# A two-block transformer kernel on one core: the order of groups in the norm stage, and where layer 0 waits for its stores of x

## Chip, cores and metric

The kernel runs on one core of a Trainium2 chip. The metric is the device time of one execution in microseconds (us), the median of several runs. One profiled execution is read for where the time goes.

## What is computed

The reference is a chain of two blocks over x, 512 rows of 1024 float32 numbers. The first block ends in a mixture of experts and a layer norm; the second has two layers (latent attention, neighbourhood attention, a gated merge, an MLP), each of which also reads keys and values of 256 context rows. Cut to what the change touches:

```
y = hierarchical_moe(x, ...)                               # two experts per row, weighed by gate
x = layer_norm(DEEPNORM_ALPHA * x + y, ln2_g, ln2_b)       # end of the first block
for l in range(DEPTH_2):                                   # two layers
    h_c = modulate(rms_norm(x_ctx, g_attn[l]), csh1, csc1)
    gl_c, mq_c, mk_c, mv_c, nq_c, nk_c, nv_c = mixer_proj(h_c, *proj_w)
    h = modulate(rms_norm(x_lat, g_attn[l]), sh1, sc1)
    ... attention over h and the context's keys and values ...
    x_lat = x_lat + gt1 * gated_merge(gl, y_mla, y_na, ...)
    h2 = modulate(rms_norm(x_lat, g_mlp[l]), sh2, sc2)
    x_lat = x_lat + gt2 * squared_relu_mlp(h2, w_ff1[l], w_ff2[l])
```

## The kernel before

Rows are tiled by 128 (P), so x has four row tiles (TT = 4). The program is a sequence of stages. In each, `products` (L233) takes a list of groups. A group is an optional batch of matmuls into one PSUM bank, and work of one engine behind it: "v" is VectorE (DVE), "s" is ScalarE (ACT), "g" is GpSimd (POOL). `products` gives every engine its own groups in the order of the list. An engine never passes a group that isn't ready, so the list's order is the order on each engine, and only counters between engines (`after`, `needs`, `reads`) say when a group may start. Within a group, `link` makes the next instruction wait for the one before it. A group with `dma=True` issues a transfer from its engine's queue; at the end of the list (L310 to L312) the engine that issued it waits until it has landed. A stage ends with a barrier of all engines.

**The norm stage** (`stream_norm`, L2687) lies between the experts and layer 0. Its list has four kinds of work.

- `combine_groups` (L2410): for each row tile t, `sums` on DVE (`add`: x times ALPHA at L2434, two multiply-adds with the gathered rows of the two experts at L2437, statistics at L2439 to L2441), `root` on ACT (L2454), and `last` on DVE (`normalise`, L2446 to L2449). POOL gathers the experts' rows (L2423), SP loads x (L2705) and the gains of the norms.
- `rms_groups` (L2509) for x: a square with its sum and a root on ACT (L2537, L2530), a scaling on DVE (L2543). Then `modulated` (L2752): 32 transposes on PE (L395), copied to `hT`, which layer 0 reads, by DVE (L2599) and ACT (L2596), and `scales` (L2719), the gains that these copies apply.
- `late_context` (L3804): layer 1's keys and values of the context rows: products on PE (L342) whose results ACT moves; the heads' norms of `k` and `nk` (L2536, L2530 on ACT; L2572, L2545, L2548 on DVE); transposes on PE (`head_transposes`, L2773, and L395) which ACT moves; and four saves to DRAM that ACT issues (L3864). It returns two parts, `early` and `late`.
- `stores`: two transfers of the normed x to `x_lat` in DRAM, issued by ACT (L2729).

POOL also writes a padded table of biases here (`pad_bias`, L3003; its copies are at L3021). The order of the list is one line, in which `spread` (L218) interleaves two lists in proportion to their lengths:

```python
products(M, "norm_p", early + spread(first + work, late) + scales + turned + stores, tiles=4, ...)
```

**The end of a layer** (`layer_output`, L3470) keeps x in the buffer `layers_yT`. After the last sums, ACT issues four stores of x to `x_lat` (L3538); the end of the list waits for their landing. The next layer's first stage is `latent_attention` (L2799), whose `stacked` (L2871 to L2873) is a small group on DVE; its scratch `squares` lies in the same `layers_yT`, and the second half of that layer loads x back from `x_lat` at L3500.

Of the kernel before, what the change touches and what calls it, by code (L numbers as in the profile page):

```python
# [16 lines left out]
ALU = mybir.AluOpType  # L17
# [7 lines left out]
TT = T // P  # L25
D = 1024
# [52 lines left out]
class Group:  # L79
# [5 lines left out]
    def __init__(self, pe, evac, on, tile=None, after=(), needs=(), other=None, pool="", reads=(), dma=False):  # L85
        self.dma = dma
        self.pe, self.evac, self.on, self.tile, self.other = pe, evac, on, tile, other
        self.after, self.needs, self.pool, self.reads = tuple(after), tuple(needs), pool, tuple(reads)
# [144 lines left out]
def products(M, name, groups, tiles=0, pools=ALL_BANKS, extra=None):  # L233
# [8 lines left out]
    for g in groups:  # L242
        if g.dma:
            g.landed = sig[f"landed{sum(x.dma for x in groups[:groups.index(g)])}"]
            continue
        tally[g.on] += 1
        g.count = tally[g.on]
        if g.pe:
            g.number = len(made)
            made.append(g)  # L250
            slots, mine = pools[g.pool], used[g.pool]
            g.before = mine[-len(slots)] if len(mine) >= len(slots) else None
            b, n = slots[len(mine) % len(slots)]
            g.bank = M.ps[:, b:b + n, :].rearrange("p b n -> p (b n)")
            mine.append(g)
            if g.tile is not None:
                W.last_group[g.tile] = base + g.number + 1
            if g.other is not None:
                W.last_group[g.other] = base + g.number + 1
# [12 lines left out]
    with nc.Block() as block:  # L272
# [22 lines left out]
        def mover(eng, on):  # L295
# [14 lines left out]
            for g in groups:  # L310
                if g.dma and g.on == on:
                    eng.wait_ge(g.landed, 16)  # L312
# [2097 lines left out]
def combine_groups(M, st, x, yg, loaded):  # L2410
# [21 lines left out]
    def add(dve, link, t):  # L2432
        dve.wait_ge(loaded(t), 16)
        link(dve.tensor_scalar(x[:, t, :], x[:, t, :], ALPHA, None, ALU.mult))  # L2434
        dve.wait_ge(sig[f"y{t}"], 32)
# [7 lines left out]
    def normalise(dve, link, t):  # L2443
# [5 lines left out]
        return dve.tensor_tensor(x[:, t, :], x[:, t, :], g[:, 1, :], ALU.add)  # L2449

    work, made, before = [], [], None
    for t in range(TT):
        sums = group(None, lambda eng, _, link, t=t: add(eng, link, t), "v")
        root = group(None, lambda eng, _, link, t=t: eng.activation(  # L2454
            rs[:, t:t + 1], mv[:, t, 1:2], ACT.Sqrt, bias=M.ln_eps[:, :]), "s", after=(sums,))
        last = group(None, lambda eng, _, link, t=t: normalise(eng, link, t), "v", after=(root,))
        work += [sums, root] + ([before] if before else [])
        before = last
        made.append((last,))
    return work + [before], made, gather, gains  # L2460

# [225 lines left out]
def stream_norm(M, layers, hT):  # L2687
# [5 lines left out]
    with Stage(nc, "norm_in") as st:  # L2693
# [4 lines left out]
        x = yg[:, 0, :, :]  # L2698
        early, late, context_load = late_context(M, st)
        first, made, gather, combine_gains = combine_groups(M, st, x_in, yg, lambda t: sig[f"x{t}"])  # L2700

# [14 lines left out]
        def gain(eng, link, l, n, out):  # L2716
            if l == 0 and n == 0:
# [5 lines left out]
                  for l, L in enumerate(layers) for n, out in ((0, L.gain1), (1, L.gain2))]  # L2723
        work, done = rms_groups(M, st, "rms", x_in, TT, 1, D, made=made, out=x,
                                share=Squares([yg[:, 1, i, :] for i in range(2)]))
# [5 lines left out]
                  for b in range(2)]  # L2731
        products(M, "norm_p", early + spread(first + work, late) + scales + turned + stores, tiles=4,
                 extra={"sync": load, "gpsimd": pool_work})

# [64 lines left out]
def latent_attention(M, L, l, hT, y, sums):  # L2799
# [9 lines left out]
    with Stage(nc, f"mla{l}") as st:  # L2809
# [61 lines left out]
        def stacked(dve, _, link):  # L2871
            dve.wait_ge(small_landed, (4 + 2 * TT) * 16)
            return dve.tensor_reduce(pick, M.ident[:, :].rearrange("p (q n) -> p n q", q=4), AX, ALU.add)  # L2873
        picked = group(None, stacked, "v")
# [595 lines left out]
def layer_output(M, layers, l, hT, y):  # L3470
# [6 lines left out]
    with Stage(M.nc, f"out{l}") as st:  # L3477
# [21 lines left out]
        final = [blocks[0][4][-1], blocks[1][4][-1]]  # L3499
        loaded = [group(None, lambda act, _, link, t=t: act.dma_start(x[:, t, :], stream_rows(M, t)), "s",  # L3500
                        reads=(final[t // 2],), dma=True) for t in range(TT)]
        complete = [(blocks[1][a][-3], blocks[1][a][-1], blocks[1][b][-3], blocks[1][b][-1]) for a, b in ((0, 2), (1, 4))]
# [31 lines left out]
        def target(t):  # L3534
            if last:
# [3 lines left out]
                        dma=True) for t in range(TT)]  # L3539
        if not last:  # L3540
            nxt = layers[l + 1]
            xn2 = flat[:, 2 * BANK:2 * BANK + TILE].rearrange("p (t d) -> p t d", d=D)
# [261 lines left out]
def late_context(M, st):  # L3804
# [37 lines left out]
    ups = []  # L3842
# [13 lines left out]
    for b in k_turned:  # L3856
# [8 lines left out]
             for dst, src, of in ((M.ctx_v[1], v[:, :, :].rearrange("p t n -> p (t n)"), ups),  # L3865
                                  (M.ctx_k[1], kT[:, :, :].rearrange("p h n -> p (h n)"), k_turned),
                                  (M.ctx_nv[1], nv[:, :, :].rearrange("p t n -> p (t n)"), vs),
                                  (M.ctx_nk[1], nkT[:, :, :].rearrange("p k n -> p (k n)"), nk_turned))]
    return kv + rest + low_work + ks + turned + ups + vs, k_work + nk_work + k_turned + nk_turned + saves, load

# [33 lines left out]
def program(nc, A, out):  # L3904
    M = Machine(nc, A, out)
    with ExitStack() as ctx:
# [41 lines left out]
        M.weights = Weights(nc, ring, tiles, slots, nc.alloc_semaphore(name="groups_done"))  # L3948
        M.scratch_L = nc.dram_tensor("scratch_L", [4, T], F32).ap()
        M.ctx_h = nc.dram_tensor("ctx_h", [P, DK * CTX], F32).ap()  # L3950
        M.x1 = nc.dram_tensor("x1_rows", [T, D], F32).ap()
# [84 lines left out]
```

## Time and profile before

| | us |
|---|---|
| median of 3 runs | 4245.66 (4245.24 to 4246.1) |
| profiled execution, its own time | 4244.85 |
| its span, first to last instruction | 4243.1 |
| PE busy | 3769.9 (89%) |
| DVE busy | 1747.2 (41%) |
| ACT busy | 757.3 (18%) |
| POOL busy | 163.2 (4%) |

The span is what the profile's rows cover; the 1.75 us beside it in the same execution lie outside the first and last instruction. Start times in the rows count from the span's start. PE is TensorE's matmul, PEld its weight load, SP the engine that issues most transfers. A busy share is an average over the whole program; in the stretches that the change touches the shares are quite different.

### The profile page before, as it was taken

The numbers are of one execution on the slowest core, as the hardware profiler recorded it, in microseconds if no ns is written. First come the engines' busy times: TensorE is split into PE (matmuls) and PEld (weight loads), VectorE is DVE, ScalarE is ACT, GpSimd is POOL, SyncE is SP. The second block draws the span as 40 slices with busy tenths as digits, with TensorE's granted clock in tenths as the row PEclk, the third lists the DMA queues.
The fourth block names the chain that finished last, engine by engine and source line by source line (L and its number), as shares of the span: only waits on it lengthen the run. The fifth ranks groups of instructions, "written<-read, shape, count | busy, mean of one in ns | idle before, by whom it ended". The sixth has DMA issues, their size and how long they took to land. (4 is left out here: it accounts for less than half of the span.)

```text
span 4243.1 us, 38455 instructions
## 1 busy us (share of the span) xinstructions
PE 3769.9 (89%) x14796; PEld 2141.4 (50%) x14796; DVE 1747.2 (41%) x3047; ACT 757.3 (18%) x1690; POOL 163.2 (4%) x377
## 2 busy tenths in 40 slices
PE   7988777799578999999866899999998899999999
PEld 3653663444344343555433555448744455447844
DVE  0128643344513211111115556355446556445545
ACT  0212201111012211000112434110001354211000
POOL 1001000000000000000020300000000300000000
PEclk9988777799689999999987999999999999999999
DMA  7443001223166768888742201132222201122221
GB/s 298 169 158 111 1 5 50 95 93 129 71 227 266 290 245 344 338 352 343 292 179 68 90 21 60 70 109 80 80 79 85 102 21 60 42 98 80 80 79 60
DMA packets 197193, 574.69 MB, mean 135 GB/s; under 512 B 24324, under 2 KB 34356, under 8 KB 183752
## 3 DMA queue, kind: packets, MB, share of 16 engines
q1 hardware_dynamic: 177704, 518.35, 32.5%
q10 hardware_dynamic: 11424, 27.37, 1.9%
q0 software_dynamic: 7888, 26.53, 1.7%
q8 instruction: 121, 1.98, 0.2%
q14 instruction: 56, 0.46, 0.0%
HBM read 540.49 MB, written 31.73 MB: 135 GB/s over the span
## 5 line engine op out<-in xcount | busy, mean ns | idle before, releaser
L342 PE MATMUL ps<-out_sums 128*128 128x256 f32 (+1 forms) x1152 | 333.6, 450 | 2.3 <-issue 2.3
L342 PE MATMUL ps<-mixers_xT,ring 128*128 128x512 f32 (+2 forms) x928 | 306.9, 491 | 1.7 <-PEq L272 0.9
L342 PEld LDWEIGHTS ps<-out_sums 128*128 128x128 f32 x1152 | 218.7, 190 | 114.2 <-issue 94.5
L342 PEld LDWEIGHTS ps<-mixers_xT,ring 128*128 128x128 f32 (+1 forms) x928 | 173.5, 188 | 130.4 <-issue 115.2
L342 PE MATMUL ps<-ring,mixers_xT 128*128 128x512 f32 (+2 forms) x608 | 222.7, 524 | 9.9 <-DVE ab_qk L336 6.1
L342 PE MATMUL ps<-ring,layers_hT 128*128 128x512 f32 x416 | 186.7, 606 | 25.5 <-PEq L272 23.5
L2205 PE MATMUL ps<-ring,moe_xgT 128*64 128x512 f32 x432 | 192.0, 601 | 3.0 <-issue 2.2
L342 PEld LDWEIGHTS ps<-ring,mixers_xT 128*128 128x128 f32 x608 | 119.9, 211 | 109.1 <-issue 94.1
L342 PE MATMUL ps<-ring,out_hidden 128*128 128x512 f32 x384 | 167.4, 592 | 0.0
L2206 PE MATMUL ps<-ring,moe_xgT 128*64 128x512 f32 x368 | 163.1, 598 | 0.0
L342 PEld LDWEIGHTS ps<-ring,layers_hT 128*128 128x128 f32 x416 | 79.6, 194 | 126.8 <-issue 122.7
L342 PE MATMUL ps<-out_hidden 128*128 128x512 f32 x288 | 125.7, 593 | 6.2 <-issue 6.2
L2205 PEld LDWEIGHTS ps<-ring,moe_xgT 128*64 128x64 f32 x432 | 58.7, 139 | 127.8 <-issue 127.8
L342 PE MATMUL ps<-layers_hT,ring 128*128 128x256 f32 x512 | 115.3, 387 | 5.1 <-ACT out_rms_rs L2530 5.1
L342 PEld LDWEIGHTS ps<-ring,out_hidden 128*128 128x128 f32 x384 | 73.0, 190 | 91.0 <-issue 90.9
L2205 PE MATMUL ps<-ring,moe_hT 128*64 128x512 f32 x224 | 100.5, 602 | 15.3 <-ACT moe_hT L334 11.3
L2243 DVE TENSOR_TENSOR moe_h<-moe_sg,ps 128x512 f32<-128x512 f32 x16 | 11.0, 688 | 246.7 <-PE ps L2206 246.7
L342 PE MATMUL ps<-ring,layers_yT 128*128 128x512 f32 x256 | 112.5, 592 | 0.0
L342 PEld LDWEIGHTS ps<-layers_hT,ring 128*128 128x128 f32 x512 | 99.5, 195 | 19.7 <-issue 5.5
L430 PE MATMUL ps<-mla_kT,mla_qT 96*128 96x512 f32 (+1 forms) x256 | 96.8, 502 | 8.1 <-ACT mla_S L444 6.6
L342 PE MATMUL ps<-ring,mla_qT 128*128 128x512 f32 (+1 forms) x256 | 94.3, 527 | 8.3 <-DVE mla_qT L2598 6.3
L342 PE MATMUL ps<-ring,ctx_ins 128*128 128x512 f32 (+1 forms) x232 | 95.8, 572 | 0.8 <-ACT ctx_ins L2595 0.8
(895 smaller groups left out, 6157.8 us busy)
## 6 DMA issues: line engine op xcount, KB each, us to landing
ring<-in_w_ff SPq DMA_DIRECT2D x45, 2048.0 KB, 12.9
ring<-in_w_in SPq DMA_DIRECT2D x40, 2048.0 KB, 12.8
ring<-in_e_down SPq DMA_DIRECT2D x27, 2048.0 KB, 8.9
ring<-in_e_gate SPq DMA_DIRECT2D x25, 2048.0 KB, 15.4
ring<-in_e_up SPq DMA_DIRECT2D x25, 2048.0 KB, 11.5
ring<-in_w_ada SPq DMA_DIRECT2D x24, 2048.0 KB, 11.6
ring<-in_w_out SPq DMA_DIRECT2D x8, 2048.0 KB, 11.4
deep_ring_more<-in_e_gate SPq DMA_DIRECT2D x8, 2048.0 KB, 16.7
```

Of the source, the lines that this page charges most:

```text
L342: last = pe.matmul(out, lhsT, rhs, start=(j == 0), stop=(j == len(pairs) - 1))
L430: last = pe_.matmul(bank[:, e * BANK + c0:e * BANK + c0 + n], q, k, start=True, stop=True)
L2205: pe.matmul(bank[0:HALF, :], left(k)[:, 0:HALF], wa[:, k, cols], **ends)
L2206: last = pe.matmul(bank[HALF:P, :], left(k)[:, HALF:P], wb[:, k, cols], **ends)
L2243: lambda eng, bank, link, i=i: eng.tensor_tensor(h[:, i, :], sg[:, i, :], bank, ALU.mult),
```

## The change

The norm stage: `late_context` now returns its parts one by one, the weighing of x by ALPHA becomes four groups of its own, and the list is written out by hand instead of by one `spread`. The number of instructions on each engine stays the same. Layer 0's four stores of x get a semaphore of their own, `M.x_stored`, and are left out of the wait at the end of the list; layer 1 waits for it in `stacked`, ahead of the first use of the buffer as scratch, and in `load_rows`, ahead of the reads of `x_lat`.

```diff
@@ __init__ of Group, products
-        self.dma = dma
+        self.dma, self.awaited = dma, None
...
-            g.landed = sig[f"landed{sum(x.dma for x in groups[:groups.index(g)])}"]
+            g.landed = g.awaited or sig[f"landed{sum(x.dma for x in groups[:groups.index(g)])}"]
...
-                if g.dma and g.on == on:
+                if g.dma and g.on == on and g.awaited is None:
                     eng.wait_ge(g.landed, 16)
@@ combine_groups
     def add(dve, link, t):
-        dve.wait_ge(loaded(t), 16)
-        link(dve.tensor_scalar(x[:, t, :], x[:, t, :], ALPHA, None, ALU.mult))
         dve.wait_ge(sig[f"y{t}"], 32)
...
+    def weigh(dve, t):
+        dve.wait_ge(loaded(t), 16)
+        return dve.tensor_scalar(x[:, t, :], x[:, t, :], ALPHA, None, ALU.mult)
...
+    weighed = [group(None, lambda eng, _, link, t=t: weigh(eng, t), "v") for t in range(TT)]
-        sums = group(None, lambda eng, _, link, t=t: add(eng, link, t), "v")
+        sums = group(None, lambda eng, _, link, t=t: add(eng, link, t), "v", after=(weighed[t],))
...
-    return work + [before], made, gather, gains
+    return weighed, work + [before], made, gather, gains
@@ stream_norm
-        early, late, context_load = late_context(M, st)
+        (low, keys, ups, values, heads, heads_turned, saves), context_load = late_context(M, st)
...
-        products(M, "norm_p", early + spread(first + work, late) + scales + turned + stores, tiles=4,
-                 extra={"sync": load, "gpsimd": pool_work})
+        scaled_, squares = [g for g in squares if g.on == "v"], [g for g in squares if g.on == "s"]
+        sums, roots, lasts = [first[i] for i in (0, 2, 5, 8)], [first[i] for i in (1, 3, 6, 9)], [m[0] for m in made]
+        work = weighed + low + keys[0:1] + [sums[0], roots[0], *scales] + keys[1:] + [sums[1], roots[1], lasts[0]] + ups
+        work += [squares[0], sums[2], roots[2], lasts[1], *heads[:3], squares[1], *values[0:1]]
+        tail = [scaled_[0], sums[3], roots[3], lasts[2], *values[1:], squares[2], scaled_[1], lasts[3], squares[3], *scaled_[2:]]
+        work += spread(tail, heads[3:]) + stores + heads_turned + saves + turned
+        products(M, "norm_p", work, tiles=4, extra={"sync": load, "gpsimd": pool_work})
@@ latent_attention, stacked
             dve.wait_ge(small_landed, (4 + 2 * TT) * 16)
+            if l:
+                dve.wait_ge(M.x_stored, 16 * TT)
@@ layer_output
-        loaded = [group(None, lambda act, _, link, t=t: act.dma_start(x[:, t, :], stream_rows(M, t)), "s",
-                        reads=(final[t // 2],), dma=True) for t in range(TT)]
+        def load_rows(act, t):
+            if l:
+                act.wait_ge(M.x_stored, 16 * TT)
+            return act.dma_start(x[:, t, :], stream_rows(M, t))
+        loaded = [group(None, lambda act, _, link, t=t: load_rows(act, t), "s", reads=(final[t // 2],), dma=True)
+                  for t in range(TT)]
...
         if not last:
+            for store in stores:
+                store.awaited = M.x_stored
@@ late_context
-    return kv + rest + low_work + ks + turned + ups + vs, k_work + nk_work + k_turned + nk_turned + saves, load
+    return (kv + rest + low_work, ks, turned + ups, vs, k_work + nk_work, k_turned + nk_turned, saves), load
```

What the list's new order does to the engines is shown at three places. PE's own sequence, POOL's and SP's are the same as before. Line numbers behind the change are its own: L2434 is now L2451, L2437 is L2435, and the rest lies some lines lower.

**Place 1: DVE from the context's low-rank norm on.** Names: `x_in` is x, `yg` the gathered experts' rows, `c_k` the context's keys, `layers_gain` the modulating gains. Before:

```order
L2543 TENSOR_SCALAR norm_in_c_ckv<-norm_in_c_ckv,norm_in_c_ckv_rs 128x256
L2434 TENSOR_SCALAR norm_in_x_in<-norm_in_x_in 128x1024
L2437 SCALAR_TENSOR_TENSOR norm_in_x_in<-norm_in_yg,gate,norm_in_x_in 128x1024 x2
L2439 BN_STATS norm_in_stats<-norm_in_x_in 128x6
L2440 BN_STATS norm_in_stats<-norm_in_x_in 128x6
L2441 BN_AGGR norm_in_mv<-norm_in_stats 128x2
L2572 TENSOR_REDUCE norm_in_c_k_ss<-norm_in_c_sq 128x8
L2434 TENSOR_SCALAR norm_in_x_in<-norm_in_x_in 128x1024
```

Now:

```order
L2451 TENSOR_SCALAR norm_in_x_in<-norm_in_x_in 128x1024 x4
L2546 TENSOR_SCALAR norm_in_c_ckv<-norm_in_c_ckv,norm_in_c_ckv_rs 128x256
L2435 SCALAR_TENSOR_TENSOR norm_in_x_in<-norm_in_yg,gate,norm_in_x_in 128x1024 x2
L2437 BN_STATS norm_in_stats<-norm_in_x_in 128x6
L2438 BN_STATS norm_in_stats<-norm_in_x_in 128x6
L2439 BN_AGGR norm_in_mv<-norm_in_stats 128x2
L2722 SCALAR_TENSOR_TENSOR layers_gain_0<-mod,norm_in_g 128x16 x2
L2722 SCALAR_TENSOR_TENSOR layers_gain_1<-mod,norm_in_g 128x16 x2
L2435 SCALAR_TENSOR_TENSOR norm_in_x_in<-norm_in_yg,gate,norm_in_x_in 128x1024 x2
```

The four weighings stand ahead of the context's low-rank norm. Behind the first tile's statistics came the sum over `c_sq`, which needs the context's keys; now the gains and the second tile follow at once.

**Place 2: ACT behind the last product `ups` of the context.** `c_nv` are values, moved from PSUM; `c_sq` with `c_k` is the square that DVE's first sum over `c_sq` needs. Before:

```order
L334 ACTIVATE norm_in_c_nv<-ps 128x512 x2
L2536 ACTIVATE norm_in_c_sq<-norm_in_c_k 128x768
L2454 ACTIVATE norm_in_ln_rs<-norm_in_mv,ln_eps 128x1
L2536 ACTIVATE norm_in_c_sq<-norm_in_c_k 128x768
L2530 ACTIVATE norm_in_c_k_rs<-norm_in_c_k_ss,eps 128x8
L2454 ACTIVATE norm_in_ln_rs<-norm_in_mv,ln_eps 128x1
L2530 ACTIVATE norm_in_c_k_rs<-norm_in_c_k_ss,eps 128x8
```

Now:

```order
L2540 ACTIVATE norm_in_yg,norm_in_rms_ss<-norm_in_x_in 128x1024
L2533 ACTIVATE norm_in_rms_rs<-norm_in_rms_ss,eps 128x1
L2457 ACTIVATE norm_in_ln_rs<-norm_in_mv,ln_eps 128x1
L2539 ACTIVATE norm_in_c_sq<-norm_in_c_k 128x768 x2
L2540 ACTIVATE norm_in_yg,norm_in_rms_ss<-norm_in_x_in 128x1024
L2533 ACTIVATE norm_in_rms_rs<-norm_in_rms_ss,eps 128x1
L334 ACTIVATE norm_in_c_nv<-ps 128x512
L2533 ACTIVATE norm_in_c_k_rs<-norm_in_c_k_ss,eps 128x8
L2457 ACTIVATE norm_in_ln_rs<-norm_in_mv,ln_eps 128x1
```

The roots and squares of the first tiles of x stand ahead of the moves of `c_nv`.

**Place 3: ACT at the end of the list.** Before:

```order
L2530 ACTIVATE norm_in_rms_rs<-norm_in_rms_ss,eps 128x1
L2595 ACTIVATE norm_in_c_nkT<-ps,norm_in_c_col_gain 128x256 x3
L3864 DMA ctx_v<-norm_in_c_v 128x1024
L3864 DMA ctx_k<-norm_in_c_kT 96x2048
L3864 DMA ctx_nv<-norm_in_c_nv 128x1024
L3864 DMA ctx_nk<-norm_in_c_nkT 128x1024
L2596 ACTIVATE layers_hT<-ps,mod,layers_gain_0 128x8x64 x4
L2729 DMA x_lat<-norm_in_x_in 256x1x1024 x2
```

Now:

```order
L2533 ACTIVATE norm_in_c_nk_rs<-norm_in_c_nk_ss,eps 128x8
L2732 DMA x_lat<-norm_in_x_in 256x1x1024 x2
L334 ACTIVATE norm_in_c_kT<-ps 96x256 x8
L2598 ACTIVATE norm_in_c_nkT<-ps,norm_in_c_col_gain 128x256 x4
L3880 DMA ctx_v<-norm_in_c_v 128x1024
L3880 DMA ctx_k<-norm_in_c_kT 96x2048
L3880 DMA ctx_nv<-norm_in_c_nv 128x1024
L3880 DMA ctx_nk<-norm_in_c_nkT 128x1024
L2599 ACTIVATE layers_hT<-ps,mod,layers_gain_0 128x8x64 x4
```

The stores of x moved ahead of the moves of the transposed heads (`c_kT`, `c_nkT`) and of the four saves; before, they were the last thing in the list (behind the copies to `layers_hT`).

## Rows read from the trace of the kernel before

**Rows 1.** Windows of the norm stage (us, busy us per engine, PE clock, DMA share, GB/s):

```profile
2220.00:2230.00 10.00, 0.00 (x0) 0.00 (x0) 9.69 (x15) 1.12 (x3) 0.00 (x0) 0.50 0.00 0
...
2280.00:2290.00 10.00, 10.00 (x24) 4.45 (x23) 6.17 (x4) 1.19 (x2) 0.00 (x0) 0.98 0.49 114
```

**Rows 2.** Timeline of DVE in the norm stage (start us, us, work, [idle before <-releaser]):

```profile
2182.57 0.69 DVE L2434 TENSOR_SCALAR norm_in_x_in<-norm_in_x_in 128x1024 f32<-128x1024 f32 x1
...
2187.25 0.21 DVE L2441 BATCH_NORM_AGGREGATE norm_in_mv<-norm_in_stats 128x2 f32<-128x12 f32 x1
2216.62 0.95 DVE L2572 TENSOR_REDUCE norm_in_c_k_ss<-norm_in_c_sq 128x8 f32<-128x768 f32 x1 [29.16 <-ACT norm_in_c_sq L2536]
...
2244.34 0.63 DVE L2572 TENSOR_REDUCE norm_in_c_nk_ss<-norm_in_c_sq 128x8 f32<-128x512 f32 x1
...
2246.57 0.15 DVE L2446 RECIPROCAL norm_in_ln_rs<-norm_in_ln_rs 128x1 f32<-128x1 f32 x1
...
2253.45 0.15 DVE L2541 RECIPROCAL norm_in_rms_rs<-norm_in_rms_rs 128x1 f32<-128x1 f32 x1
...
2256.90 0.42 DVE L2719 SCALAR_TENSOR_TENSOR layers_gain<-mod,norm_in_g 128x16 f32<-128x16 f32 x4
```

**Rows 3.** Timeline of PE, norm stage and start of layer 0:

```profile
2230.88 3.65 PE L2773 MATMUL ps<-ident,norm_in_c_k 128*96 128x128 f32 x16 [15.66 <-DVE norm_in_c_k L2548]
...
2257.38 6.61 PE L395 MATMUL ps<-ident,norm_in_yg 128*128 128x128 f32 x32 [8.64 <-DVE layers_gain L2719]
2276.38 15.98 PE L342 MATMUL ps<-ring,layers_hT 128*128 128x512 f32 x32 [12.39 <-PEq L272]
```

**Rows 4.** Timeline of ACT and its queue (ACTq) in the norm stage:

```profile
2192.95 0.60 ACT L334 ACTIVATE norm_in_c_nk<-ps 128x512 f32<-128x512 f32 x1 [6.27 <-PE ps L342]
...
2202.14 0.39 ACT L334 ACTIVATE norm_in_c_v<-ps 128x256 f32<-128x256 f32 x1
...
2246.19 1.05 ACT L2537 ACTIVATE norm_in_yg<-norm_in_x_in 128x1024 f32<-128x1024 f32 x1
...
2247.57 0.36 ACT L334 ACTIVATE norm_in_c_kT<-ps 96x256 f32<-96x256 f32 x1
...
2256.70 1.93 ACTq L3864 DMA_DIRECT2D ctx_nk<-norm_in_c_nkT  x1
...
2262.80 2.50 ACT L2596 ACTIVATE layers_hT<-ps,mod,layers_gain 128x512 f32<-128x512 f32 x2 [0.42 <-PE ps L395]
2264.03 1.27 ACTq L2729 DMA_DIRECT2D x_lat<-norm_in_x_in  x2
```

**Rows 5.** Loads of the modulating gains (L2709): instruction form and time to landing:

```profile
L2709 SPq DMA_DIRECT2D norm_in_g<-in_g_mlp x2: 554/882/1209, 2167.7 to 2169.0; - x2
...
DMA to landing us min/median/max: 18.5/18.6/18.7
```

**Rows 6.** Landing of the two stores of x (L2729), and a window during them:

```profile
DMA to landing us min/median/max: 7.1/9.0/11.0
...
2269.00:2270.00 1.00, 0.00 (x0) 0.00 (x0) 0.00 (x0) 0.00 (x0) 0.00 (x0) 0.50 1.01 205
```

**Rows 7.** Landing of the four saves of the context (L3864):

```profile
DMA to landing us min/median/max: 2.8/6.1/6.8
```

**Rows 8.** POOL beside DVE: bias copies; four small operations alone; the same four beside DVE:

```profile
2187.03 4.61 POOL L3021 COPY norm_in_rpb_runs<-norm_in_rpb 8x248 f32<-8x248 f32 x8 [12.65 <-DMA norm_in_rpb<-in_rpb]
...
2357.24 1.15 POOL L2558 TENSOR_TENSOR layers_yT<-mla_heads,mla_rope 128x64 f32<-128x64 f32 x4
...
2365.44 2.58 POOL L2558 TENSOR_TENSOR layers_yT<-mla_heads,mla_rope 128x64 f32<-128x64 f32 x4 [4.22 <-DVE mla_heads L2548]
```

**Rows 9.** From layer 0 to layer 1: ACT's queue, SP's queue, landing of the stores (L3538):

```profile
3259.02 2.02 ACTq L3538 DMA_DIRECT2D x_lat<-layers_yT  x2
...
3265.17 2.94 SPq L2838 DMA_DIRECT2D mla_rope<-in_rope_cos  x4
...
DMA to landing us min/median/max: 2.6/4.0/4.8
```

More of the change, by code:

```diff
@@ L2698, in stream_norm @@
         x = yg[:, 0, :, :]
-        early, late, context_load = late_context(M, st)
-        first, made, gather, combine_gains = combine_groups(M, st, x_in, yg, lambda t: sig[f"x{t}"])
+        (low, keys, ups, values, heads, heads_turned, saves), context_load = late_context(M, st)
+        weighed, first, made, gather, combine_gains = combine_groups(M, st, x_in, yg, lambda t: sig[f"x{t}"])
         def load(sp):
@@ L2723, in stream_norm @@
                   for l, L in enumerate(layers) for n, out in ((0, L.gain1), (1, L.gain2))]
-        work, done = rms_groups(M, st, "rms", x_in, TT, 1, D, made=made, out=x,
+        squares, done = rms_groups(M, st, "rms", x_in, TT, 1, D, made=made, out=x,
                                 share=Squares([yg[:, 1, i, :] for i in range(2)]))
@@ L3949, in program @@
         M.scratch_L = nc.dram_tensor("scratch_L", [4, T], F32).ap()
+        M.x_stored = nc.alloc_semaphore(name="x_stored")
         M.ctx_h = nc.dram_tensor("ctx_h", [P, DK * CTX], F32).ap()
```

## The prediction, made before the changed kernel ran

> **What bounds the kernel now.** I read the page first: PE is busy 89% of the span, so only places where PE stands still can give much. The windows of the norm stage show one: from 2220 to 2230 us PE does nothing while DVE is busy 9.69 of 10 us [rows 1]. The timeline of DVE then shows two halves of this stage. After the first tile's statistics, which end at 2187.46, DVE stands idle 29.16 us, until ACT has squared the context's keys; from 2216.62 on it has no pause until the gains end at 2257.32 [rows 2]. So the work on x sits behind a group that becomes ready late, although its data isn't missing. PE's transposes of x begin behind it, at 2257.38, and layer 0's products at 2276.38 [rows 3]. What fills the time between the last copy of the transposes (2265.3 [rows 4]) and 2276.38 is the landing of the two stores of x: the second is issued at 2264.7 and lands at most 11.0 us later, 2275.7 [rows 4, 6], 0.7 us ahead of PE. The second place is the end of layer 0: ACT's last issue ends at 3261.04, the slowest landing took 4.8 us, and the next stage begins at 3265.17 [rows 9].
>
> **DVE's chain in the new order.** No work is removed. DVE's work in the stage behind the context's low-rank norm is what it does without a pause from 2216.62 to 2257.32, 40.7 us, and the first tile's, 4.9 us from 2182.57 to 2187.46 [rows 2]: 45.6. The four weighings (0.69 each [rows 2], 2.8) go ahead of it, into time in which DVE waited anyway: 42.8 remain. Two waits come in. The gains stand behind the first tile's sums, at 2182.57 + 4.2 = 2186.8; their last load is issued at 2169.0 and takes 18.7 [rows 5], so DVE waits until 2187.7, 0.9 us. The first sum over the context's squares then comes behind three tiles' sums (4.2 each), two normalisations (3.44 each, from 2246.57 to 2253.45 for two [rows 2]) and the gains (0.4): at 2203.4. ACT is later: it ends the moves of the context's values at 2202.53 [rows 4], I add 0.3 for a root that now stands ahead of them behind the move at 2192.95, then comes a square of x (1.4, from 2246.19 to 2247.57 [rows 4]), a root and a square of the keys (together about 1.0): 2205.2. DVE waits 1.8. The chain ends at 2182.57 + 42.8 + 0.9 + 1.8 = 2228.1, and I take 2228.5 for a third, short wait for ACT's last square.
>
> **PE and ACT behind it.** The context's last transposes are 8, at 16 in 3.65 us [rows 3] 1.8 us: 2230.3. Then the transposes of x, 6.6 us [rows 3]: 2236.9, against 2264.0 before. PE stays at the lower clock there in both kernels, as the 0.50 in the window says [rows 1].
>
> **The transfers decide the end.** Behind the last normalisation DVE has left two scalings (0.86 each, from 2253.45 to 2256.90 for four), and a sum and two scalings of `c_nk` (2.2, from 2244.34 to 2246.57) [rows 2], and the short wait: the last tile of x is normed at about 2224.2, ACT's square and root of it end at 2225.9, and then ACT issues the stores. Alone they took 11.7 us from the first issue (2264.03) to the last landing (2275.7), and the 16 DMA engines were full meanwhile (1.01 at 205 GB/s) [rows 4, 6]. So they land at 2237.6. The four saves are issued from about 2231, into full engines. Before, they took from about 2255.0 to 2256.70 + 6.8 = 2263.5 at most, 8.5 us [rows 4, 7]; less 1 us of start, which overlaps, 7.5 go behind the stores: 2245.1. ACT's own four copies to `hT` (1.25 each, 5.0 [rows 4]) come behind the issue of the saves, the last of which took 1.93 us [rows 4]. That issue may stretch while the queue is full, at most until the stores have landed: 2237.6 + 5.0 = 2242.6, still ahead of the transfers. From landing to PE's first product it was 0.7 us: 2245.8 against 2276.4, **30.6 us earlier**. Bounds: if stores and saves share the engines better than one behind the other, ACT's copies end the stage at the earliest, 2231 + 3.6 of issues + 5.0 = 2239.6, and the gain is 36. The other bound is the next item.
>
> **DVE beside POOL.** DVE works where it stood idle, and there POOL copies biases, 8 copies in 4.61 us, twice [rows 8]. Where both are busy in layer 0, the same four small operations of POOL took 2.58 us instead of 1.15 [rows 8]. So they do hinder each other, and the row shows POOL paying. POOL has time: 16 copies, each as much as 1 us later, end near 2226, long before 2245. For DVE the trace gives no price in this stage. It is between nothing and all of POOL's copies, 2 x 4.61 = 9.2 us; I take 1.0, since the nearest row shows POOL as the one that waits. The Trainium skill (SBUF — State Buffer, Who interferes with whom) says that the pair of ports which the two share is locked for a whole instruction, and that whoever starts first makes the other block. By that rule DVE pays for each copy that gets in first, in the worst order the 9.2 us; the slower small operations agree with a lock, and no row decides who would start first here.
>
> **The end of layer 0.** Four stores are no longer awaited there. Their issue remains: ACT is done at 3261.04 [rows 9]. What is left is the barrier. From the latest landing (3259.0 to 3259.8 + 4.8, so 3263.8 to 3264.6) to the start at 3265.17 it was 0.6 to 1.4 us [rows 9]. So layer 1 starts at 3261.6 to 3262.4, 2.8 to 3.6 us earlier; I take 3.3 and 2.0 as the lower bound, since the stores now share the engines with layer 1's first loads. The two waits that come in cost nothing. `stacked` stands in layer 1's list behind 16 us of products (before layer 0 the first of them took 15.98 [rows 3]), and the loads of x stand in a later stage, while the stores land within 5. If that cover were gone, DVE's queue would wait for at most the 4.8 us of the landing.
>
> **Sum.** 30.6 - 1.0 + 3.3 = 32.9 us. Layer 0 and layer 1 shift whole: their weights are asked for as PE gives slots back, and the window behind layer 0's start shows the DMA engines half busy, 0.49 [rows 1]. Against the profiled execution's own 4244.85 that is 4212.0; it stands 0.8 below the median of 4245.66. From the median it is 4212.8, and I forecast **4213**.
>
> **Rivals.**
> 1. *Stores and saves overlap, ACT's copies end the stage:* gain 36 and 3.6, 4206. For it: 205 GB/s at full engines is no high rate [rows 6], and no row shows both kinds of transfer at once. Against it: 1.01 of the engines is full.
> 2. *DVE pays for POOL's copies* in full, 9.2 us instead of 1.0, and the boundary gives its lower bound: 4213 + 8.2 + 1.3 = 4222.5. The lock of the page named above is this case. For it: DVE has hardly a gap between 2187 and 2229. Against it: in the nearest rows it is POOL that waits.
> 3. *The change moves the wait without shortening it:* a load of weights further on takes back what layer 0 gains, so that the end moves by less than 8 us: about 4240. For it: the last of the ring's loads before layer 0 are as early as before, in either kernel. Against it: PE at 2276.38 waited for the barrier and for no transfer [rows 3], and later loads hang on PE's own progress.
> 4. *Slower, by PE's clock:* layer 0 starts earlier but at the lower of the two levels, 1.2 instead of 2.4 GHz, and stays there. Each us of dense products at that level costs half a us, so the 32.9 us are lost after 66 us at 0.50; with 90 us it would be 4258. For it: the clock is 0.50 all through the stretch before [rows 1], and PE does less in it than before. Against it: before, it was back at 0.98 within 4 us of layer 0's start [rows 1, 3], after just such an idle stretch.
>
> **How the numbers follow.** Forecast 0.80; rival 1 0.07; rival 2 0.07; rival 3 0.03; rival 4 0.02; 0.01 for what I don't see. The range reaches from rival 1 to rival 2, 4206 to 4223, both the bounds of the unknown costs; it leaves out rivals 3 and 4 and the edges of the others. Within 0.2% (8.5 us, about what a measurement of this kernel can tell from no change) lies rival 3; forecast and rivals 1 and 2 are faster. Faster 0.95, same 0.03, slower 0.02.
>
> **What would show it.** In the new profile DVE's idle of 29 us is gone, with two waits of 1 to 2 us in its place; the chain ends near 2228; PE transposes x from about 2230; the stores of x are issued near 2226, and PE's first product of layer 0 is at 2245 to 2247 with SP just ahead of it. Between the first products of layer 0 and of layer 1 nothing but the 3.3 us changes. I am wrong if layer 0 starts after 2250, if the last thing before it is a compute instruction rather than a landing, or if its first 10 us are at 0.50.

## The result and the profile after

| | before | after |
|---|---|---|
| median of the runs beside each other, us | 4245.45 (4242.62 to 4246.1, 4 runs) | 4216.83 (4213.43 to 4219.15, 4 runs) |
| ratio, 95% interval | | 0.9933 (0.9916 to 0.995) |
| the profiled execution's own time, us | 4244.85 | 4215.68 |
| its span, us | 4243.1 | 4213.8 |

The kernel is 28.6 us faster by the medians, 29.3 by the spans; 32.9 were forecast, and the time lies in the range. A second measurement at the end, six runs, gave 4215.52 and a ratio of 0.9932 (0.992 to 0.9944).

I cut both spans at the same five instructions: the first load of the norm stage, PE's first product of layer 0, the end of ACT's last store of layer 0, PE's first product of layer 1, the end.

| us | before | after | saved |
|---|---|---|---|
| up to the norm stage's first load | 2160.82 | 2162.35 | -1.5 |
| norm stage | 115.56 | 86.27 | 29.3 |
| layer 0 to its last store's issue | 984.66 | 986.84 | -2.2 |
| from there to layer 1 | 4.37 | 0.80 | 3.6 |
| layer 1 | 977.69 | 977.54 | 0.15 |

DVE's timeline in the norm stage, after (columns as in [rows 2]):

```profile
2173.64 3.43 DVE L2451 TENSOR_SCALAR norm_in_x_in<-norm_in_x_in 128x1024 f32<-128x1024 f32 x2 [33.77 <-DMA norm_in_x_in<-x_rows]
...
2188.99 1.31 DVE L2722 SCALAR_TENSOR_TENSOR layers_gain<-mod,norm_in_g 128x16 f32<-128x16 f32 x4 [0.84 <-DMA norm_in_g<-in_g_mlp]
2190.23 3.25 DVE L2435 SCALAR_TENSOR_TENSOR norm_in_x_in<-norm_in_yg,gate,norm_in_x_in 128x1024 f32<-128x1024 f32 x2
...
2198.36 2.60 DVE L2435 SCALAR_TENSOR_TENSOR norm_in_x_in<-norm_in_yg,gate,norm_in_x_in 128x1024 f32<-128x1024 f32 x2
...
2204.70 1.54 DVE L2447 TENSOR_TENSOR norm_in_x_in<-norm_in_x_in,norm_in_ln 128x1024 f32<-128x1024 f32 x1
2206.66 0.95 DVE L2575 TENSOR_REDUCE norm_in_c_k_ss<-norm_in_c_sq 128x8 f32<-128x768 f32 x1 [0.42 <-ACT norm_in_c_sq L2539]
...
2208.39 3.23 DVE L2435 SCALAR_TENSOR_TENSOR norm_in_x_in<-norm_in_yg,gate,norm_in_x_in 128x1024 f32<-128x1024 f32 x2
...
2230.00 0.69 DVE L2548 TENSOR_TENSOR norm_in_c_nk<-norm_in_c_nk,norm_in_c_nk_rs 128x512 f32<-128x512 f32 x1
```

The first two weighings take 3.43 us instead of 2 x 0.69 while POOL clears its table beside them (2173.32 to 2175.92): the first takes 2.83 and ends 0.55 us behind POOL. They stand ahead of the chain, and DVE waits for the next rows behind them anyway. The wait of 29.16 us for the context's squares [rows 2] is now 0.42. The same pair of L2435 takes 2.60 when DVE is alone and 3.23 to 3.25 while POOL copies; the statistics in the same stretches (L2437, L2438) keep their 0.69 and 0.68. POOL pays as well: 8 copies took 4.61 [rows 8], now, in its timeline,

```profile
2188.45 6.66 POOL L3031 COPY norm_in_rpb_runs<-norm_in_rpb 8x248 f32<-8x248 f32 x8 [12.53 <-DMA norm_in_rpb<-in_rpb]
...
2203.81 8.86 POOL L3031 COPY norm_in_rpb_runs<-norm_in_rpb 8x248 f32<-8x248 f32 x8 [2.09 <-DMA norm_in_rpb<-in_rpb]
```

Then ACT and its queue, and PE, after; they answer to [rows 3, 4]:

```profile
2227.75 0.60 ACTq L2732 DMA_DIRECT2D x_lat<-norm_in_x_in  x1
...
2233.14 2.15 ACTq L3880 DMA_DIRECT2D ctx_k<-norm_in_c_kT  x1
2235.34 2.44 ACTq L3880 DMA_DIRECT2D ctx_nv<-norm_in_c_nv  x1
2237.82 1.93 ACTq L3880 DMA_DIRECT2D ctx_nk<-norm_in_c_nkT  x1
2239.80 4.33 ACT L2599 ACTIVATE layers_hT<-ps,mod,layers_gain 128x512 f32<-128x512 f32 x4 [6.57 <-issue]
```

```profile
2232.51 4.30 PE L395 MATMUL ps<-ident,norm_in_yg 128*128 128x128 f32 x32
2248.62 16.79 PE L342 MATMUL ps<-ring,layers_hT 128*128 128x512 f32 x32 [11.81 <-PEq L272]
```

ACT's copies end at 2244.13, PE begins at 2248.62. The window from 2229, where the first store's bytes begin to move, to 2246 (columns as in [rows 1]), and the landings of the stores of x and of the saves:

```profile
2229.00:2246.00 17.00, 6.06 (x40) 5.82 (x40) 5.93 (x9) 8.37 (x16) 0.00 (x0) 0.70 0.97 258
```

```profile
DMA to landing us min/median/max: 7.1/9.8/12.4
...
DMA to landing us min/median/max: 9.3/10.7/12.3
```

And of the last save, `ctx_nk`, alone:

```profile
DMA to landing us min/median/max: 10.1/10.1/10.1
```

The DMA engines are busy for 0.97 of 17 us. `ctx_nk`, issued at 2237.82, lands at 2247.9, and PE begins 0.7 us later, just as it did behind the last store of x before (2275.7 and 2276.38 [rows 3, 4, 6]). The transfers end the stage, as they did before; they only begin earlier.

The end of layer 0 (ACT's queue; SP's; PE), after, against [rows 9]:

```profile
3233.44 2.02 ACTq L3552 DMA_DIRECT2D x_lat<-layers_yT  x2
```

```profile
3236.02 3.44 SPq L2846 DMA_DIRECT2D mla_rope<-in_rope_cos  x4
```

```profile
3236.26 9.34 PE L342 MATMUL ps<-ring,layers_hT 128*128 128x512 f32 x16 [3.82 <-PEq L272]
```

SP goes on 0.56 us behind the last issue (3235.46) instead of 4.13, while the slowest store still takes 5.9 us to land.

### The profile page after: what moved, and what is told of

Read it like the earlier page. It is cut to its first block and busy times, and to the rows that moved or that the text cites. A ratio compares the mean times of both kernels' runs of the same rounds, so it can differ in the third digit from the quotient of the medians.

```text
span 4213.8 us, 38458 instructions
## 1 busy us (share of the span) xinstructions
PE 3772.1 (90%) x14796; PEld 2140.0 (51%) x14796; DVE 1751.3 (42%) x3047; ACT 756.8 (18%) x1690; POOL 169.5 (4%) x377
```

## The experiments

Ten more kernels ran, one execution each; `thirds` and the kernel after were then timed again. "Norm stage" and the other stages are cut as in the table above; times counted from the stage's first load are written +66.0. Single executions scatter by some us (before alone: 4238.6 to 4253.4 in the last eleven runs), so I read the stages and not the total where less than 5 us matter.

| kernel | time, us | span | norm stage | layer 0 | to layer 1 |
|---|---|---|---|---|---|
| order_only | 4216.54 | 4214.6 | 86.55 | 986.61 | 4.35 |
| stores_only | 4239.58 | 4237.8 | 115.59 | 984.78 | 0.80 |
| stores_last | 4213.01 | 4211.2 | 89.00 | 984.26 | 0.80 |
| weigh_back | 4213.87 | 4212.0 | 88.96 | 987.99 | 0.80 |
| early_stores | 4222.18 | 4220.3 | 99.10 | 984.41 | 0.78 |
| saves_pool | 4210.85 | 4209.1 | 86.81 | 986.72 | 0.81 |
| no_pad | 4213.19 | 4211.2 | 86.96 | 986.73 | 0.76 |
| stores_up | 4239.25 | 4237.5 | 112.82 | 984.07 | 4.34 |
| halves | 4203.19 | 4201.3 | 81.14 | 982.65 | 0.77 |
| thirds | 4203.26 | 4201.5 | 77.21 | 985.85 | 0.81 |
| thirds_timed | 4205.50 (5 runs) | 4200.9 | 77.86 | 984.67 | 0.77 |
| after_timed | 4215.52 (6 runs) | 4216.7 | 86.28 | 987.19 | 0.76 |

**The two parts, each alone.** order_only is the kernel after without its way of awaiting layer 0's stores:

```diff
-            for store in stores:
-                store.awaited = M.x_stored
-            if l:
-                dve.wait_ge(M.x_stored, 16 * TT)
-            if l:
-                act.wait_ge(M.x_stored, 16 * TT)
```

> The new order of the norm stage alone; layer 0's stores of x are awaited at the list's end again. If the two parts are independent: from the first load of the norm stage to PE's first product of layer 0 it takes 86.3 us as in the changed kernel (115.6 before), and from ACT's last issue of layer 0 to PE's first product of layer 1 4.4 us as before (0.8 in the changed kernel). Rival: the second part depends on the first (both queues of stores share the engines with what follows), then the 4.4 us come out over 1 us different. Total about 3.6 us over the changed kernel's, plus or minus 3 by the clock.

stores_only is the kernel before with those lines and the new attribute `awaited` alone.

> The kernel before with layer 0's stores awaited where layer 1 needs them. Norm stage 115.6 us as before; 0.8 us from ACT's last issue to PE's first product of layer 1. Rival: without the wait the stores share the engines with layer 1's first loads, and layer 1's first groups on DVE come later than before, counted from the stage's start, so that part of the 3.6 us is given back; then the first 100 us of layer 1 are over 1 us longer.

The norm stage is 86.55 with the order and 115.59 without; the boundary 4.35 without the awaiting and 0.80 with it. Each part does its share by itself, 29.0 and 3.6 us, and they don't touch each other. PE's first products of layer 1, in order_only and in stores_only:

```profile
3237.43 7.92 PE L342 MATMUL ps<-ring,layers_hT 128*128 128x512 f32 x13 [7.38 <-PEq L272]
```

```profile
3260.17 8.25 PE L342 MATMUL ps<-ring,layers_hT 128*128 128x512 f32 x13 [3.84 <-PEq L272]
```

**Inside the order.** stores_last puts the stores of x back to the end of the list, behind the transposes of x:

```diff
-        work += spread(tail, heads[3:]) + stores + heads_turned + saves + turned
+        work += spread(tail, heads[3:]) + heads_turned + saves + turned + stores
```

> The changed kernel with the two stores of x back at the end of the norm stage's list, behind ACT's copies to hT. Theory A (the gain comes from DVE's order, and the stores' place only overlaps the transfers): ACT copies end near 2241, the stores are issued then and take 11.7 us, PE starts layer 0 about 4 us later than in the changed kernel, 90 to 91 us after the first load. Theory B (the gain is the overlap of the stores' landing with work): most of the 29.3 us is lost, over 105 us.

weigh_back puts each weighing right before its tile's sums, as it stood before:

```diff
-        work = weighed + low + keys[0:1] + [sums[0], roots[0], *scales] + ...
+        work = low + keys[0:1] + [weighed[0], sums[0], roots[0], *scales] + ...
```

> The changed kernel with each weighing of x again right ahead of its tile's sums. Theory A: DVE's chain bounds the stage, so the four times 0.7 us come back on it; the first is partly hidden, PE starts layer 0 2 to 3 us later (88 to 89 us). Rival: the chain has slack because transfers end the stage; then they move with the last tile's store all the same unless the saves alone bound it: no change within 0.5 us.

stores_up is the kernel before with one line changed, the stores of x ahead of the gains and of the transposes of x:

```diff
-            spread(first + work, late) + scales + turned + stores,
+            spread(first + work, late) + stores + scales + turned,
```

> The kernel before with the two stores of x ahead of the gains and of x's transposes, behind the saves, and nothing else. Theory A: the gain of the place alone is the overlap of the stores with transposes and copies, PE starts layer 0 about 5 us earlier than before, 109 to 112 us after the first load (115.6). Theory B (the place is the cause of most of the gain): under 100 us.

Each of the three is worth 2.7 us (89.00, 88.96, and 112.82 against 115.56). For stores_last that is 1 us less than expected, for stores_up 0.8 us short of the expected range. So of the 29.3 us, 2.7 come from where the stores stand, 2.7 from the weighings in time that DVE spent waiting (four of 0.69 each), and the rest, some 24 if the three add, from DVE's remaining order, which was not taken apart further. That the stores' place is worth so little with DVE's chain shortened is because the saves fill the DMA engines in the stores' stead: stores_last issues its last save 3.3 us earlier (+72.21 against +75.47) and the second store of x 10 us later (+76.04 against +66.04), and its last landing is 2.7 us later (+88.3 against +85.6). In its ACT rows the issue of the stores also overlaps ACT's copies without holding them:

```profile
2231.63 2.03 ACTq L3880 DMA_DIRECT2D ctx_nk<-norm_in_c_nkT  x1
2233.70 1.26 ACT L2599 ACTIVATE layers_hT<-ps,mod,layers_gain 128x512 f32<-128x512 f32 x1 [3.29 <-PE ps L395]
2234.27 1.15 ACTq L2732 DMA_DIRECT2D x_lat<-norm_in_x_in  x1
```

**Does DVE pay for POOL's copies (rival 2)?** no_pad leaves the copies of the bias rows out (the padded table then holds only zeros), and with them everything POOL computes beside DVE's chain (its clearing of the table, ahead of the chain, stays):

```diff
-            for r in range(ROWS):
+            for r in range(0):
```

> The changed kernel without POOL's 16 copies of biases in the norm stage (left out, so that the bias table holds zeros). If POOL's copies cost DVE what its longer instructions show (gains 1.3 instead of 0.4 us, three others 0.3 to 0.65 more each, 2.5 us in all), DVE's chain and with it the stores and PE's first product come 2 to 2.5 us earlier (84 us). Rival: the longer instructions are slowed by transfers or by the table of clocks, not by POOL: no change.

Alone, DVE's rows are short again, and its wait for ACT has grown:

```profile
2186.12 0.43 DVE L2722 SCALAR_TENSOR_TENSOR layers_gain<-mod,norm_in_g 128x16 f32<-128x16 f32 x4 [0.65 <-DMA norm_in_g<-in_g_mlp]
2186.47 2.60 DVE L2435 SCALAR_TENSOR_TENSOR norm_in_x_in<-norm_in_yg,gate,norm_in_x_in 128x1024 f32<-128x1024 f32 x2
...
2203.75 0.95 DVE L2575 TENSOR_REDUCE norm_in_c_k_ss<-norm_in_c_sq 128x8 f32<-128x768 f32 x1 [2.25 <-ACT norm_in_c_sq L2539]
```

In the kernel after, POOL costs DVE 0.88 on the gains, 0.65, 0.32 and 0.63 on the rows shown: 2.5 us. Of these 1.8 only take the place of the wait for ACT (0.42 against 2.25), so x is stored 0.55 us earlier without them (+65.49 against +66.04). The stage isn't shorter at all (86.96; 84 was expected): the last save lands 11.3 us behind its issue instead of 10.1, at +86.3 instead of +85.6. Why it does so stays open. Rival 2 is out: the price is real, a quarter of its bound, and nearly all of it was covered.

**What ends the stage?** early_stores meant to spread the transfers: one store for each tile of x as soon as it is normed, and each save as soon as its data is there.

```diff
-        stored = M.x_lat.rearrange("(c t b) d -> b c t d", b=2, t=TT)
-        stores = [... act.dma_start(stored[b], x_in[b * GRID_W:(b + 1) * GRID_W, 0:TT, :]), ... for b in range(2)]
+        stored = M.x_lat.rearrange("(c t b) d -> t b c d", b=2, t=TT)
+        stores = [... act.dma_start(stored[t], x_in[:, t, :]), ... after=made[t] ... for t in range(TT)]
```

> The changed kernel with the transfers out of the norm stage's tail: the stores of x are four, one per row tile, issued as each tile is normed, and three of the four saves are issued as soon as their data is ready. If transfers end the stage (stores and saves one behind the other, 20 us from the first issue to the last landing), then only one store and one save (512 KB each) are left behind 2228, ACT's copies to hT or the last landing end near 2239, and PE starts layer 0 about 77 us after the stage's first load, 9 us earlier than in the changed kernel (86.3). Rival: the stage is ended by DVE's chain and ACT's copies, or ACT's queue is held up by each issue: then under 4 us.

It missed by 22 us. ACT's queue, DVE and a window of it:

```profile
2215.95 11.38 ACTq L3883 DMA_DIRECT2D ctx_nv<-norm_in_c_nv  x1
2227.38 0.30 ACT L2533 ACTIVATE norm_in_c_nk_rs<-norm_in_c_nk_ss,eps 128x8 f32<-128x8 f32 x1 [11.33 <-issue]
```

```profile
2231.81 0.16 DVE L2544 RECIPROCAL norm_in_rms_rs<-norm_in_rms_rs 128x1 f32<-128x1 f32 x1 [7.87 <-ACT norm_in_rms_rs L2533]
```

```profile
2220.00:2226.00 6.00, 1.30 (x7) 0.83 (x5) 3.87 (x5) 0.00 (x0) 0.00 (x0) 0.50 0.13 53
```

While only stores of the new form were under way, the engines' share was 0.13, at 53 GB/s, where the stores of the kernel after fill them at 200. A share of 0.13 is that of two busy engines out of 16, and 2 is also the outer size of the new destination (`b`), where the other stores have 64 (`c`); that the one follows from the other was not tested. The issue behind them held ACT for 11.38 us, and DVE with it (7.87 us). The stage's last landing, of `ctx_nk`, comes at 2256.6, 19.6 us behind its issue instead of 10.1, and 0.7 us ahead of PE. So this run says nothing on early stores as such, only on this form: all 128 partitions of one tile, in one transfer, to rows interleaved in pairs.

saves_pool lets POOL issue the four saves; the first line is needed for POOL to run a list of transfers alone:

```diff
-            if tally["g"]:
+            if any(g.on == "g" for g in groups):
...
-            ... act.dma_start(dst, src), "s", after=of, dma=True)
+            ... act.dma_start(dst, src), "g", after=of, dma=True)
```

> The changed kernel with the four saves issued by POOL instead of ACT. ACT's copies to hT no longer wait behind issues that take 2 us each, and end about 6 us earlier (77.5 + 4.3 us after the first load in the changed kernel). If the transfers end the stage, layer 0 still starts at 86.3 us, within 1 us; if ACT's blocked issue does, it starts up to 6 us earlier.

POOL, ACT and windows of it:

```profile
2228.90 0.54 POOL L3880 DMA_DIRECT2D ctx_nk<-norm_in_c_nkT  x1 [0.82 <-ACT norm_in_c_nkT L2598]
```

```profile
2229.67 4.38 ACT L2599 ACTIVATE layers_hT<-ps,mod,layers_gain 128x512 f32<-128x512 f32 x4 [1.06 <-PE ps L395]
```

```profile
2236.00:2238.00 2.00, 0.00 (x0) 0.00 (x0) 0.00 (x0) 0.00 (x0) 0.00 (x0) 0.54 0.98 352
2238.00:2240.00 2.00, 0.00 (x0) 0.00 (x0) 0.00 (x0) 0.00 (x0) 0.00 (x0) 0.50 0.73 285
```

ACT's copies end 5.2 us earlier (+76.57 against +81.78), the last save is issued 4 us earlier, and the stage lasts 86.81, as before. In its last 10 us no engine computes. So neither ACT nor the issues set the end: from the first store of x the engines have some 17 us of work (2 MB of x at 200 GB/s, 10.5, and 2.25 MB of saves at about 350, 6.7). In saves_pool `ctx_v` went out 11 us ahead of the stores, and the last landing is 0.9 us earlier than in the kernel after (+84.7 against +85.6). That is lost again behind it. `ctx_nk`, the last save, and PE's first products in saves_pool:

```profile
DMA to landing us min/median/max: 13.3/13.3/13.3
```

```profile
2244.29 16.70 PE L342 MATMUL ps<-ring,layers_hT 128*128 128x512 f32 x32 [12.04 <-PEq L272]
```

It lands at 2242.2, and PE begins 2.1 us later. The same two distances stand in every run: from the stage's last landing to PE it is 0.7 us in the nine kernels where ACT issued that transfer and waits for it, and 2.1 us in saves_pool, halves and thirds, where POOL does. So POOL's part in the end of the stage costs 1.4 us. saves_pool was fast in its time (4210.85) only because its norm stage began 4.9 us earlier than that of the kernel after, which the change doesn't touch.

**Work moved ahead of the full stretch.** halves is saves_pool with `ctx_nv` saved ahead of `ctx_k`, and with the stores of x split by tiles, each still from 64 partitions:

```diff
-        stores = [... act.dma_start(stored[b], x_in[b * GRID_W:(b + 1) * GRID_W, 0:TT, :]), ...
-                  for b in range(2)]
+        stores = [... act.dma_start(stored[b][:, lo:hi, :], x_in[b * GRID_W:(b + 1) * GRID_W, lo:hi, :]), ...
+                  after=sum(made[lo:hi], ()), dma=True)
+                  for lo, hi in ((0, 2), (2, TT)) for b in range(2)]
-        work += [..., *heads[:3], squares[1], *values[0:1]]
+        work += [..., *heads[:3], squares[1], *stores[0:2], *values[0:1]]
-        work += spread(tail, heads[3:]) + stores + ...
+        work += spread(tail, heads[3:]) + stores[2:] + ...
```

> The kernel after with the four context saves issued by POOL (as in the earlier run), ctx_nv ahead of ctx_k, and the two stores of x cut in four: rows of tiles 0 and 1 behind squares[1], rows of tiles 2 and 3 where both stood; each still takes one half of the partitions. Theory (once DVE's chain is short, the stage's end is set by the DMA engines, busy without a gap from the first store of x to the last save, about 17 us; only work moved ahead of that stretch shortens it): 1 MB of x (5.2 us at the 200 GB/s of the stores) moves to about 2204 to 2210 and ctx_nv (1.5 us) ahead too; the stretch starts at the same place and is 10 us long; the norm stage lasts 80 to 82 us instead of 86.3 to 86.8, time about 4205, span 4203 to 4206. Rival A (the last copies of the transposed x, or POOL's last landing, end the stage whatever the engines do): no shorter than 84.5 us, time 4208 or more. Rival B (any store of x ahead of the norm's end slows DVE or blocks ACT's queue, as the per-tile stores did): DVE's chain over 1 us longer than in the run with POOL's saves, ACT's issue over 2 us, time 4212 or more.

thirds splits them at `((0, 2), (2, 3), (3, TT))`, with the middle two behind `squares[2]`.

> The kernel of the run before with tile 2's rows of x in two stores of their own behind squares[2] (512 KB), so that only tile 3's rows (512 KB, 2.6 us at 200 GB/s) are left for the end. Theory: another 2.6 us off the stretch, norm stage 77.5 to 79.5 us, span 4200 to 4203, unless the copies of the transposed x (which ended 76.6 us behind the first load when POOL had the saves) come last: then 79 to 80. Rival A: same as the run before it within 0.5 us. Rival B (stores of one row of 4 KB for each of 64 partitions are as slow as the per-tile ones, 53 GB/s): the DMA share in their stretch is 0.2 to 0.3 and the stage is longer than in the run before it, over 84 us.

Norm stages of 81.14 and 77.21 us: the theory's numbers for the first (80 to 82), 0.3 below them for the second, whose step is 3.9 us instead of 2.6. Both rivals are out; a store of one row of 4 KB for each of 64 partitions still moves at full speed. In thirds: PE, a window behind ACT's last work but one, and the landing of the last save, which POOL issued at 2231.37:

```profile
2230.36 4.39 PE L395 MATMUL ps<-ident,norm_in_yg 128*128 128x128 f32 x32
2237.39 13.09 PE L342 MATMUL ps<-ring,layers_hT 128*128 128x512 f32 x26 [2.64 <-PEq L272]
```

```profile
2235.00:2237.00 2.00, 0.00 (x0) 0.00 (x0) 0.86 (x1) 1.56 (x2) 0.00 (x0) 1.00 0.00 0
```

```profile
DMA to landing us min/median/max: 3.9/3.9/3.9
```

The last save lands at 2235.3, and PE starts 2.1 us behind it, once more. ACT's last copy ends at 2236.56, 0.8 us ahead of PE, with the DMA engines empty. In the second trace of thirds that distance is 1.4 us, and the one from the landing is 2.1 again. So the landing that POOL waits for still ends the stage, and compute comes close behind it. Such stores with ACT issuing the saves were not tried.

**The faster version timed, beside the kernel after.**

> The kernel thirds again, timed in five rounds against the kernel before. By its stages (norm stage 77.2 against 115.6, boundary 0.8 against 4.4, layer 0's own time 1 to 3 us longer where the clock falls behind PE's pause, layer 1 the same) 38.4 + 3.6 - 1.5 = 40.5 us less than before: 4203 to 4206 us, ratio 0.990 to 0.991. Rival (the short stage of one profile was a lucky one, other runs are like the run with POOL's saves alone): 4210.

> The kernel after unchanged, timed beside the one above on the same chip, so that what its own median (4216.8, single times from 4213.4 to 4219.2) holds of chance is known. Theory: its stages say 29.3 + 3.6 - 2.2 = 30.7 less than before by the profile, so 4213 to 4217. The run above is 9 to 12 us faster. Rival (the second measurement lies as high as the first single times): 4218 or more.

Both times hold; the ratio of thirds_timed is just above the expected 0.991. thirds_timed: 4205.50 us, ratio to before 0.9915 (0.9902 to 0.9927). after_timed: 4215.52 us, 0.9932 (0.992 to 0.9944). The norm stages differ by 8.4 us, the medians by 10.0. Single runs of one kernel differ by 8 us and more (after: 4210.85 to 4218.85; before by up to 15), so the difference of the medians is good to some us only; the stages say what it is made of.

## Why the prediction was right, and where its numbers were off

Before the change, the last landing of a transfer ended the norm stage, and DVE's chain decided when the transfers could begin. The forecast's steps, in its order, times again from the stage's first load (2160.82 before, which the forecast's times imply; 2162.35 after):

1. *DVE's chain.* It was to end at 2228.5, with 1.0 for POOL beside it 2229.5, which is +68.7; it ended at 2230.69, +68.34. Two terms were off and nearly cancel: the price for POOL was 2.5 instead of 1.0, and the wait for ACT's squares 0.42 instead of 1.8. They aren't independent: a slower DVE arrives later and waits less. The prediction added them as if they were. no_pad shows the exchange. That the chain came out within 0.4 us is in part luck.
2. *PE's transposes of x.* Forecast from 2230.3 for 6.6 us; measured +70.16 (the forecast's 2230.3 and 1.0 are +70.5), and 4.30 us. The prediction held PE at its lower clock here; the granted clock was 0.81 over 2230 to 2240 in the kernel after and 1.00 at the end of the transposes. It cost nothing, as PE doesn't end the stage.
3. *Stores of x.* Forecast at 2225.9 and 1.0 later, +66.1; the first was issued at 2227.75, +65.40.
4. *Stores, then saves.* Forecast for PE 19.9 us behind the stores' first issue (2225.9 to 2245.8), measured 20.9 (2227.75 to 2248.62). The picture of two loads one behind the other on full engines is what the window shows (0.97 busy). The long issues of the saves (2.15, 2.44, 1.93) and ACT's copies behind them, until 2244.13, stayed under it; that is +81.78, just the prediction's bound of 2242.6. saves_pool settles that they cost nothing.
5. *Rival 1* (stores and saves overlap, 4206) is refuted by the same run: with ACT free and all saves issued by 2229.44 the stage isn't shorter. With ACT's 0.7 us behind the last landing in place of POOL's 2.1 it would be 0.9 us shorter, an estimate from the two distances above; rival 1 had 5 to 6.
6. *Layer boundary.* 3.3 forecast, 3.57 measured, nearly the upper of the two bounds (2.8 to 3.6), and the new waits in layer 1 show nothing (layer 1: 977.69 and 977.54).
7. *Rivals 3 and 4.* No later load takes anything back, and the clock doesn't stay low. But the claim that layer 0 shifts whole was wrong by 2.2 us, and that is the larger part of the miss. 0.8 lie in its first products (16.79 against 15.98 [rows 3]; the granted clock over their first 10 us is 0.72 against 0.80). Another 3.0 are lost at one place, behind a pause of PE that both kernels have, and 1.7 are won back some 40 us later, where the clock falls in the kernel before instead. For the first place PE and a window around it, after, then before:

```profile
2787.61 16.95 PE L342 MATMUL ps<-out_hidden 128*128 128x512 f32 x32 [3.09 <-issue]
```

```profile
2780.00:2800.00 20.00, 16.91 (x45) 8.12 (x44) 11.74 (x13) 2.39 (x4) 0.00 (x0) 0.83 0.05 17
```

```profile
2814.49 13.97 PE L342 MATMUL ps<-out_hidden 128*128 128x512 f32 x32 [3.09 <-issue]
```

```profile
2808.00:2828.00 20.00, 16.91 (x52) 8.31 (x51) 12.16 (x13) 2.39 (x4) 0.00 (x0) 1.00 0.00 0
```

For the second, a window of the same work, after, then before:

```profile
2818.62:2838.62 20.00, 17.45 (x75) 12.52 (x74) 15.80 (x23) 5.79 (x12) 0.00 (x0) 1.00 0.58 210
```

```profile
2846.38:2866.38 20.00, 17.46 (x76) 13.91 (x75) 12.71 (x17) 5.79 (x12) 0.00 (x0) 0.91 0.59 210
```

At the first place the same 32 products after the same pause of 3.09 us take 3 us more, since the granted clock falls in one kernel and not in the other. So rival 4's mechanism exists, at a twentieth of the size it was given. It isn't tied to the edit alone: layer 0 took 984.3 in stores_last, which has the new order too, 987.99 in weigh_back, and 982.65 in halves, whose first 32 products take 13.97 us, at full clock from the start. Why the clock falls in one and not in the other stays open.

The rest of the miss is 1.5 us ahead of the norm stage, which no line of the change touches; the stage's first load lies between 2156.84 and 2165.00 in these runs. Sum: norm stage 29.3 against 29.6 forecast, boundary 3.6 against 3.3, layer 0 -2.2, ahead of it -1.5, layer 1 0.15, together 29.3.

## What to carry to other kernels

A list of groups in fixed order should be read for the one that becomes ready late: 29 us of one engine's idle time went away by order alone. Once the chain is short, ask what its end releases: here two stores and four saves at one moment, 17 us of full DMA engines, so the next 9 us came from sending what was ready earlier. Take a transfer that is sent early in the form that is known to fill the engines, since a badly spread one blocks the queue that issues it, and the engine behind that queue. Look too at who waits for the last landing: here the step from it to the next stage took 0.7 us with ACT and 2.1 with POOL.

## What the runs showed of the hardware

- A store of 512 KB in the form [128 partitions, one row of 4 KB], to rows interleaved in pairs, moved 53 GB/s at 0.13 of the engines, the share of two out of 16 (early_stores); the same rows as two stores from 64 partitions each moved about 200 GB/s and filled them (thirds). Behind the first form the issue of the next transfer held ACT for 11.38 us.
- ACT's issues of the four saves took 0.34, 0.44, 0.78 and 1.93 us with nothing ahead of them (before), and 0.34, 2.15, 2.44 and 1.93 behind the two stores of x (after); POOL's issues of the same saves took 0.52 to 0.58 in either case (saves_pool, halves, thirds).
- From the last landing to PE's first product of the next stage it took 0.7 us where ACT issued the last transfer, 2.1 where POOL did (saves_pool, halves, thirds and its second trace).
- DVE and POOL slow each other: DVE's pair of 128x1024 operations went from 2.60 to 3.25 us, POOL's eight copies from 4.61 to 6.66 and 8.86. The Trainium skill (SBUF — State Buffer, Who interferes with whom) has the one that comes second blocked for a whole instruction. The trace agrees in kind: both sides lost, POOL 6.3 us over 16 copies and DVE 2.5, and one weighing (2.83 us instead of 0.69) ended just behind POOL's clearing of the table. By the worst order of that rule DVE would have lost 9.2 to the copies, an estimate.
- At full engine share the rate was 200 GB/s for the stores of x and about 350 GB/s for the context's saves (windows of 2 us in saves_pool: 201 and 352). A busy share alone doesn't say how fast the bytes go.
